# Two-layer hybrid diffusion block: one gate-rank projection, attention output per head, waits per chunk, x loaded in halves, a biased exponent on ScalarE, a paced plan

## The reference, cut to what matters

```
h  = rmsnorm(x, g1) * (1 + sc1) + sh1                 # sc1, sh1: silu(c) @ ada_w + ada_b
z  = h @ w_in   -> pool, q, k, v, r, lr_f(16), lr_b(16), q_dn, kv_dn, k_rope, gates
log_gate(lr, d) = log_sigmoid(lr @ gate_w[d] + gate_b[d]) / 16      # d = forward, backward
gla, per chunk of 64 tokens:
    b = cumsum(g);  qe = q exp(b);  ke = k exp(-b);  kd = k exp(b_last - b)
    o = mask(qe ke^T) v + qe S;   S = exp(b_last) S + kd^T v
mla: softmax((qn kn^T + qr kr^T) * scale) v          # 8 heads; latents read 512 keys, context 256
x  = x + g1 * (sigmoid-gated sum of three branches @ w_out)
h2 = rmsnorm(x, g2) * (1 + sc2) + sh2
peer: q = h2 @ wq; scores against 2 x 128 keys; top 16 of 16 x 16; for each token and head
      16 experts:  sum_j softmax_j * gelu(h2 . u[e_j]) * v[e_j]
x  = x + g2 * peer
```

## Time and profile before

| what | value |
|---|---|
| median of 3 runs | 3509.55 us (3503.07 to 3510.31) |
| the profiled execution: its own time, its span | 3512.18 us, 3510.2 us |
| PE busy | 2868.5 us (82%) |
| DVE, ACT, POOL busy | 1751.3 us (50%), 1083.8 us (31%), 862.1 us (25%) |
| moved | 1071.64 MB, mean 305 GB/s, of which the gathers 805.36 MB |
| mean granted clock of TensorE | 0.890 |
| chain that ended last | PE 53%, DMA 26%, DVE 10%, ACT 6% |

### The profile page before, as it was taken

How to read it: one execution, slowest core, us unless ns; L and a number is a source line. 1 busy time by engine, 2 the same in 40 slices (tenths; PEclk the granted TensorE clock), 3 DMA queues, 4 the chain that set the end, 5 groups by cost and what they waited for, 6 DMA issues and landing times.

```text
span 3510.2 us, 42731 instructions
## 1 busy us (share of the span) xinstructions
PE 2868.5 (82%) x16338; PEld 1793.2 (51%) x16338; DVE 1751.3 (50%) x4345; ACT 1083.8 (31%) x3065; POOL 862.1 (25%) x772
## 2 busy tenths in 40 slices
PE   7999998988898999988776555699999985566555
PEld 5787887654555666664332111278888741111111
DVE  1323013557676555556676766423300256667664
ACT  1222102243555444323433323222310123222232
POOL 0000000323233333323334444200000034444442
PEclk9999999999999999999877867799999987767776
DMA  8654441988898999989989999732144199999996
GB/s 324 273 204 157 156 152 61 379 345 337 347 373 325 420 416 421 384 338 365 386 327 410 415 410 414 300 120 87 70 155 147 72 376 415 411 411 410 410 412 278
DMA packets 151107, 1071.64 MB, mean 305 GB/s; under 512 B 16564, under 2 KB 18228, under 8 KB 22520
## 3 DMA queue, kind: packets, MB, share of 16 engines
q0 software_dynamic: 110592, 805.36, 57.0%
q1 hardware_dynamic: 40312, 263.56, 19.6%
HBM read 1067.80 MB, written 1.05 MB: 304 GB/s over the span
## 4 chain that ended last, share of the span: by engine, by line
PE 53%; DMA 26%; DVE 10%; ACT 6%; issue 3%; POOL 2%; DVEq 0%; ACTq 0%; SPq 0%; POOLq 0%
PE bank L388 39%; DMA ring<-in_experts,eid 25%; PE bank L402 11%; DVE ring L1357 5%; POOL ring L1782 2%; ACT topk_work L909 1%; PE bank L484 1%; ACT topk_work L902 1%; ACT topk_work L899 1%; PE bank L415 1%; DVE state L1547 1%; ACT L899 1%; ACT h_even L967 0%; DVE topk_work L1327 0%; PE bank L608 0%
## 5 line engine op out<-in xcount | busy, mean ns | idle before, releaser
L1782 POOL DMA_INDIRECT ring<-in_experts,eid x768 | 861.9, 1122 | 2611.1 <-PE bank L402 1317.2
L402 PE MATMUL bank<-ring,topk_work 64*64 64x512 f32 x6144 | 992.8, 775 | 542.9 <-ACT topk_work L909 539.1
L1357 DVE CUSTOM_DVE_ANT_0 ring<-ring,h2tok 128x1024 f32<-128x1024 f32 x768 | 936.6, 1224 | 591.7 <-DMA ring<-in_experts,eid 583.4
L402 PEld LDWEIGHTS bank<-ring,topk_work 64*64 64x64 f32 x6144 | 237.3, 160 | 1189.7 <-ACT topk_work L909 888.3
L899 ACT ACTIVATE topk_work<-topk_work 128x2 f32<-128x2 f32 x384 | 77.9, 203 | 1153.1 <-DVE topk_work L1357 1152.5
L388 PE MATMUL bank<-h_even,weights 128*128 128x256 f32 (+1 forms) x1360 | 313.8, 390 | 11.7 <-ACT h_even L967 11.7
L388 PEld LDWEIGHTS bank<-h_even,weights 128*128 128x128 f32 (+1 forms) x1360 | 252.0, 187 | 79.1 <-issue 26.4
L388 PE MATMUL bank<-h_odd,weights 128*128 128x256 f32 (+1 forms) x1056 | 241.5, 385 | 0.8 <-DVE h_even L1566 0.8
L909 ACT ACTIVATE topk_work<-const,topk_work 128x64 f32<-128x64 f32 x768 | 226.0, 341 | 0.4 <-ACT topk_work L902 0.4
L388 PEld LDWEIGHTS bank<-h_odd,weights 128*128 128x128 f32 (+1 forms) x1056 | 196.2, 189 | 57.1 <-issue 26.9
L902 ACT ACTIVATE topk_work<-topk_work 128x1 f32<-128x1 f32 x768 | 184.6, 287 | 12.6
(11 more groups left out here) (230 smaller groups left out, 3096.3 us busy)
## 6 DMA issues: line engine op xcount, KB each, us to landing
weights<-in_quads SPq DMA_DIRECT2D x150, 1024.0 KB, 7.6
ring<-in_quads SPq DMA_DIRECT2D x85, 1024.0 KB, 4.8
ring<-in_experts,eid POOLq DMA_INDIRECT x768, 8.7
ring<-in_quads SPq DMA_DIRECT2D x6, 768.0 KB, 4.2
weights<-in_quads SPq DMA_DIRECT2D x6, 768.0 KB, 6.1
weights<-in_quads SPq DMA_DIRECT2D x12, 256.0 KB
xT<-in_xT SPq DMA_DIRECT2D x1, 2048.0 KB, 11.0
out<-h_even SPq DMA_DIRECT2D x1, 1024.0 KB, 4.5
```

The lines of the kernel that those rows point to most:

```text
L402: x = nc.tensor.matmul(acc[g][out, :], diag[mine, J % 4, :], ring[mine, J % RING, D + h * 512:D + (h + 1) * 512], start=first, stop=J % TI ...
L1357: v.tensor_tensor_reduce(row, row, h2tok[:, u // UNITS % 2, :], 1.0, 0.0, ALU.mult, ALU.add, dots[:, u % 2, j:j + 1]).then_inc(S["dot_done ...
L1782: pool.indirect_dma_start(ring[:, J % RING, :], None, d["experts"], bass.IndirectOffsetOnAxis(eid[:, u % 2, j:j + 1], 0)).then_inc(gathere ...
```

## The change

- **Gate ranks.** The 32 rank columns of both directions are projected as one job, and the gate weights have 33 rows, with zeros for the other direction.
- **Attention.** The order of steps is head by head, both tiles of a head after each other. `weigh` takes one head and both tiles, 256 columns, on every second step; `att_out` copies 256 columns.
- **Waits.** The projection of the ranks and `turn_h2` wait for each chunk of `h` before its own matmul, not for all 8 first.
- **x.** The context half of x is loaded first; the latents' half comes after the 8 modulation quads. The modulation's scale quads (2, 3) come before its shift quads (0, 1), and DVE scales between them.
- **Gla.** ACT copies b_last / 16 to `ends` and takes exp(-b/16 + ends) itself in 8 instructions of 64 columns, straight from PSUM. DVE's copy and subtraction go.
- **State.** For latents (s = 1) the last update of the state of each direction (units 2 and 3, second half) is left out, since nothing reads it.
- **Plan.** `pace` is 0.1 from the start of pass 1 to its queries.

```diff
-PACE = 1.0
+BESIDE, PACE = 0.1, 1.0
-MOD_FIRST = [(0, q) for q in range(4)]
+MOD_FIRST = [(0, q) for q in (2, 3, 0, 1)]
+        ends = sb("ends", [P, 3, GLA_H, 2])
-        lr17 = E[0:RANK + 1, 2560:3072].rearrange("p (d t) -> p d t", d=2)
+        ranks = E[0:2 * RANK + 1, 2560:2816]
         def att_units():
-            return [(t, h) for t in range(2) for h in range(MLA_H)]
+            return [(t, h) for h in range(MLA_H) for t in range(2)]
+        def increments(s, u):
+            return 1 if s and u >= 2 else 2
# SP
-            sp.dma_start(XT[:], ...)
+            sp.dma_start(XT[:, :, span(0)], xT[:, :, span(0)]).then_inc(x_landed, 16)
+            for order, (key, n, slot, done) in enumerate(quads_of):
+                if order == 2 * len(MOD_FIRST):
+                    sp.dma_start(XT[:, :, span(1)], xT[:, :, span(1)]).then_inc(x_landed, 16)
# PE
                     for k in range(nk):
+                        if ready:
+                            pe.wait_ge(*at("h", ready, n, k))
-                    for m in range(2):
+                    for m in range(increments(p.s, u)):
-                def weigh(m): ... x = mm(b[:, 0:P], v, probT[m % 2][:, k, :], ...)
+                def weigh(h):
+                    for t in range(2):
+                        pe.wait_ge(*at("evicted", "pt", n, 2 * h + t))
+                    b = job("ao", n, h)
+                        x = mm(b[:, 0:TS], v, probT[h % 2][:, k, :], k == 0, k == nk - 1)
-                    if m >= 1:
-                        weigh(m - 1)
+                    if m and m % 2 == 0:
+                        weigh(m // 2 - 1)
-                for k in range(DC):
-                    pe.wait_ge(*at("h", "norm1", n, k))
-                project(n, "lr", w, [(0, 0, RANK), (1, RANK, RANK)], h_of(n), DC)
+                project(n, "lr", w, [(0, 0, 2 * RANK)], h_of(n), DC, ready="norm1")
                     for c in range(4):
+                        if t == 0:
+                            pe.wait_ge(*at("h", "norm2", GROUP_PASS[g], m * 4 + c))
-                            cur["pace"] = PACE if g == 1 else 0.0
+                            cur["pace"] = (0.0, PACE, 0.0)[g]
+                if n == 1:
+                    cur["pace"] = BESIDE
# ACT
+                    if p.n == 0 and name == "norm1" and c % 4 == 0:
+                        act.wait_ge(*at("evicted", "mod", 0, 2 * SH1 + c // 4))
-                    act.wait_ge(*at("bdiff", n, u))
-                    nc.scalar.activation(gla_buf(u, GD), gla_buf(u, GD), ACT.Exp, scale=1.0 / TAU)
+                    nc.scalar.activation(ends[...], last_of(b, u), ACT.Copy, scale=1.0 / TAU)
+                    act.wait_ge(*at("ends", n, u))
+                    for h in range(GLA_H):
+                        for c in range(2):
+                            mine = slice(c * CHUNK, (c + 1) * CHUNK)
+                            x = nc.scalar.activation(gla_buf(u, GD)[:, h, mine], bv[:, h, mine], ACT.Exp,
+                                                     scale=-1.0 / TAU, bias=ends[:, u % 3, h, c:c + 1])
# DVE
-                def scale_keys_first(u): ... L1494, L1497, before carry(u - 1, 0)
+                    rows_before("b", n, u)          # in scale_keys, then the wait for ACT
-                        carry(u - 1, 1)
+                        if increments(s, u - 1) == 2:
+                            carry(u - 1, 1)
-                    if m >= 1:
-                        att_out(m - 1)
+                    if m and m % 2 == 0:
+                        att_out(m // 2 - 1)
-                    for i, q in MOD_FIRST:
+                    for i, q in MOD_FIRST[:2]:
                         mod_out(i, q)
                     dve.wait_ge(*at("amod", 0, 0))
                 scale_rows("norm1", 0, p, rstd1[:, :])
+                    for i, q in MOD_FIRST[2:]:
+                        mod_out(i, q)
```

More of the change, by code:

```diff
@@ L230, in build @@
         prob = E[:, 0:1024].rearrange("p (n t) -> p n t", n=2)
-        probT = (E[:, 1024:1536].rearrange("p (k t) -> p k t", k=4), E[:, 1536:2048].rearrange("p (k t) -> p k t", k=4))
+        probT = [E[:, m:m + 1024].rearrange("p (k t) -> p k t", k=4) for m in (1024, 2048)]
         merge_tmp = E[:, 0:512].rearrange("p (n t) -> p n t", n=2)
@@ L324, in _ @@
             sp.dma_start(vec[:], d["vec"]).then_inc(const_landed, 16)
-            sp.dma_start(XT[:], d["xT"].rearrange("(c p) t -> p c t", p=P)).then_inc(x_landed, 16)
+            xT = d["xT"].rearrange("(c p) t -> p c t", p=P)
+            sp.dma_start(XT[:, :, span(0)], xT[:, :, span(0)]).then_inc(x_landed, 16)
             last, loads = {}, {}
-            for key, n, slot, done in quads_of:
+            for order, (key, n, slot, done) in enumerate(quads_of):
+                if order == 2 * len(MOD_FIRST):
+                    sp.dma_start(XT[:, :, span(1)], xT[:, :, span(1)]).then_inc(x_landed, 16)
                 if slot in last:
@@ L454, in square_sums, with project @@
                 return b
-            def project(n, name, w, chunks, src, nk, rows=True):
+            def project(n, name, w, chunks, src, nk, rows=True, ready=None):
                 for c, off, m in chunks:
@@ L609, in turn @@
                     full(x, "pt", n, m)
-                def weigh(m):
-                    t, h = au[m]
-                    pe.wait_ge(*at("evicted", "pt", n, m))
-                    b = job("ao", n, m)
+                def weigh(h):
+                    for t in range(2):
+                        pe.wait_ge(*at("evicted", "pt", n, 2 * h + t))
+                    b = job("ao", n, h)
                     for k in range(nk):
                         v = (VVctok if k < 2 else VVltok)[:, k % 2, h * MV:h * MV + MV]
-                        x = mm(b[:, 0:P], v, probT[m % 2][:, k, :], k == 0, k == nk - 1)
-                    full(x, "ao", n, m)
+                        x = mm(b[:, 0:TS], v, probT[h % 2][:, k, :], k == 0, k == nk - 1)
+                    full(x, "ao", n, h)
                 pe.wait_ge(*at("evicted", "krd", n))
@@ L642, in gate_logits @@
                 w = quad(i, "gate", k=2)
+                pe.wait_ge(*at("evicted", "lr", n, 0))
                 for dd in range(2):
-                    pe.wait_ge(*at("evicted", "lr", n, dd))
                     for t in range(2):
                         b = job("z", n, dd, t)
-                        x = mm(b[:, :], lr17[:, dd, tokl(t)], w[:, dd, :], True, True)
+                        x = mm(b[:, :], ranks[:, tokl(t)], w[:, dd, :], True, True)
                         full(x, "z", n, dd, t)
@@ L815, in queries @@
                 breathe(8.0)
-                for k in range(DC):
-                    pe.wait_ge(*at("h", "norm2", n, k))
                 if g == 1:
@@ L1075, in mixer @@
                     copy_out(kvd[:, c, :], b[:, 0:TS], "kvd", n, c)
-                act.wait_ge(*at("full", "s", n, 2, 1, 1))
+                act.wait_ge(*at("full", "s", n, 2, increments(s, 2) - 1, 1))
                 if p.full:
@@ L1157, in turned @@
                     b = bank_of("pt", n, m)
-                    if m >= 2:
-                        act.wait_ge(*at("full", "ao", n, m - 2))
-                    copy_out(probT[m % 2][:, 0:nk, :], b[:, 0:nk * P].rearrange("p (k t) -> p k t", k=nk), "pt", n, m)
+                    h, t = divmod(m, 2)
+                    if h >= 2 and t == 0:
+                        act.wait_ge(*at("full", "ao", n, h - 2))
+                    copy_out(probT[h % 2][:, 0:nk, tokl(t)], b[:, 0:nk * P].rearrange("p (k t) -> p k t", k=nk), "pt", n, m)
                 expo(0)
@@ L1459, in mixer @@
                 n, i, s = p.n, p.i, p.s
-                v.memset(lr17, 1.0).then_inc(*mark("dve_step", ("lr1", n)))
+                v.memset(ranks, 1.0).then_inc(*mark("dve_step", ("lr1", n)))
                 dve.wait_ge(*at("lr1", n))
-                for dd in range(2):
-                    b = bank_of("lr", n, dd)
-                    copy_out(lr17[0:RANK, dd, :], b[0:RANK, 0:TS], "lr", n, dd)
+                b = bank_of("lr", n, 0)
+                copy_out(ranks[0:2 * RANK, :], b[0:2 * RANK, 0:TS], "lr", n, 0)
                 beside(n, "lr")
@@ L1577, in mixer @@
                         mask(u)
-                    if 0 < u < len(units) - 1:
-                        scale_keys_first(u + 1)
                     if u >= 1:
@@ L1876, in layout @@
         put((i, "lr"), tiled(w[:, 4096:4128]))
-        put((i, "gate"), np.concatenate([a["gla_gate_w"][i], a["gla_gate_b"][i][:, None, :]], 1).transpose(1, 0, 2))
+        gate = np.zeros((2 * RANK + 1, 2, GLA_H * DK), np.float32)
+        for dd in range(2):
+            gate[dd * RANK:(dd + 1) * RANK, dd] = a["gla_gate_w"][i][dd]
+            gate[2 * RANK, dd] = a["gla_gate_b"][i][dd]
+        put((i, "gate"), gate)
         for name, first, count in (("p", 0, 4), ("q", 1024, 2), ("k", 1536, 2), ("v", 2048, 4), ("r", 3072, 4)):
```

44 lines of the change are left out of this document (17 added, 27 removed).

## The result

The changed kernel took 3472.79 us (median of 4 runs, 3470.91 to 3475.70) against 3507.91 for the kernel before (4 runs, 3503.07 to 3510.31) beside it: ratio 0.9896, 95% interval 0.9875 to 0.9918, some 35 us faster. Forecast was 3487, range 3467 to 3506. Run again in experiment 5, the same kernel took 3478.75, ratio 0.9922, 0.9901 to 0.9943. The two intervals overlap; by the two ratios the gain is 27 to 36 us.

What follows compares the result with a forecast made beforehand. PE's own sequence was taken to bound passes 0 and 3, PE and DMA both nearly full beside rows, gathers where rows run alone. Terms summed to -22.3 us: 3490 from the profiled 3512.2, 3487 against the median; range 3467 to 3506.

Steps and rivals of the forecast that it cites:

- Opening, -8.0 forecast: Start of pass 0: ranks start 6.0 us earlier, fewer rank matmuls save 3.5, slow clock costs 1.5; bounds -6 and -12.
- the term for the clock: Opening: more work falls into the 1.2 GHz time at 32 to 46 us, costing 1.5 us.
- the prediction's signs of being wrong: x's first half after 10 us, clock low until 50 us, or PE's diagonal waits in pass 1 up over 15 us.
- Attention of pass 0, +2.0: Two attention steps take 4.02 us for 3.76, eight times, so 2.0 us are lost; bounds 0 and +3.
- Gla, +0.3 and -0.6: Moving the exponents to ScalarE loses 0.3 us in pass 0 and gains 0.6 in pass 3; bounds -2 and +2.
- Norm2, -1.5 twice: Waits per chunk let 7 of 8 transposes finish early, gaining 1.5 us each in pass 0 and at pass 3's end.
- Pass 3, -7.6 from norm1 to norm2: Pass 3: ranks and norm1 gain 6.5 us, gla 0.6 and attention 0.5.
- Pass 1, -4: Beside rows in pass 1: 3 us gained by work removed, 1 by the plan; the plan's bounds are -12 and +15.
- the plan -1: Pass 1: `pace` moves about one pair of rows forward out of the merge, gaining 1 us.
- the slower rival: Pass 1: pace moves 4 to 5 pairs that stall PE, losing 32 us, total 3525; chance 0.08, half of it slower.
- the faster one: Pass 1: pace pays, earlier rows fill idle DMA and 14 us more go, total about 3471; chance 0.14.
- Pass 2, -2: Pass 2: the ranks' 3.5 us go where PE has 70 us idle, gaining 2 us; bounds -5 and +3.

Runs made afterwards that it cites:

- experiment 5: The changed kernel run again unchanged, beside the kernel before: 3478.75 us, ratio 0.9922.
- experiment 7: The kernel before with only the biased exponents on ScalarE added: 3495.32 us, ratio 0.9977 against the kernel before.
- experiment 12: The kernel before with the single rank job, biased exponent on ScalarE and left-out state updates: 3487.79 us, ratio 0.9953 against the kernel before.
- experiment 1: The changed kernel with a pace of 0 instead of 0.1 beside pass 1: 3482.03 us, ratio 0.9943 against the kernel before.
- experiment 8: The changed kernel with x loaded in one transfer, new quad order kept: 3477.71 us, ratio 0.9932 against the kernel before.
- experiment 9: The changed kernel with the four modulation quads in the old order 0, 1, 2, 3: 3476.62 us, ratio 0.9913 against the kernel before.

## Why the prediction was right, point by point

- **Opening, -8.0 forecast.** The first k matmul came 11.7 us earlier (10.8 to 11.9 in the six other executions with all of the opening's parts), not 8.0. The ranks start 7.1 us earlier for 6.0, and from there to k 4.6 us are gained for 2.0. The mechanism was right; the term for the clock was wrong in sign. I gave +1.5 because more work would fall into the slow time at 32 to 46. The slow time moved with the work, to 25.4 to 35.6, and was 10.2 us for 13.7. Of the parts: the rank job 2.1 (51.24 to 49.11 between experiments 7 and 12, in spite of 6.8 us more slow clock), and everything else, 8.1 (49.1 to 41.0), hangs on waits and order together. Each alone recovers most: without the new order 0.9 is lost, without the waits by chunk 2.7. Halves of x are 0.7. None of the prediction's signs of being wrong showed: x's first half was there by 9.2 us (10), the clock was back at 35.6 (50), and PE's waits for the diagonals in the first part of pass 1 went from 48.9 to 50.3 us (15 more).
- **Attention of pass 0, +2.0.** +2.2, with the forecast's steps to the hundredth (2.29; 1.70 for 1.73).
- **Gla, +0.3 and -0.6.** Between 0 and -1.7 in pass 3 (experiment 7). Eight exponents take 1.75 us, my low end was 2.0. They are 1.2 us more than the one of 512 columns (0.59), where the smaller estimate that the prediction mentions had 0.4 more.
- **Norm2, -1.5 twice.** -1.7 in place at pass 3's end. In pass 0 from scaling to the first gather 28.2 us are left for 27.7 when half the slow time is taken off: nothing reached the rows.
- **The whole of pass 0** to the first gather: forecast -7.2. Measured -15.9, of which 8.5 is the clock (30.7 us slow before, 13.7 after, at half cost); -7.4 is left. That the sum came out is partly luck: the opening gave some 2 us more than forecast even with its own clock taken off, norm2 gave 2 less. And the two profiled executions differ by as much again in clock.
- **Pass 3, -7.6 from norm1 to norm2.** -5.2 in the profiled execution; 494.9 us, -7.4, in experiments 1, 5, 8 and 9. Slow clock is 6.8 us before, 9.1 changed and 3.4 in those four; less half of it, -6.3 and -5.7. Up to the reciprocal of gla's norms: 177.6 before, 174.4 with the ranks and the exponent (experiment 12), 169.3 with the waits too (experiments 1, 5, 8 and 9); with slow clock of 6.8, 10.2 and 3.4 us in them, a part of each step is the clock. The ranks' copy 6.5 earlier was exact. The term for the attention, -0.5, was +0.9. I had read PE as the bound from one step in the middle, which has no gap. In the last two steps PE waits for the other engines, 2.0 us before and 3.1 changed.
- **Pass 1, -4.** Measured is 0 (881.5 to 881.3 us less half the slow time), so the step that failed would be "the plan -1" and with it "-3 work off PE". But single executions lie in 876.5 to 885.7 by this measure, too wide to tell 0 from -4. The rows moved further than I planned: the last gather came 853.6 us after the first, and 853 us after its own first gather the kernel before stood at gather 247 of 256, so it is four to five pairs and not one. Neither rival's price came: no stall (the slower rival), nothing paid (the faster one). The rows ended early, and norm2, the queries and the choice of rows of the latents were the last wait.
- **Pass 2, -2.** The term that was mis-sized most: -11 (mean of ten against four), with the traces pointing at VectorE's queue in gla. I counted 3.5 us of PE's time at a little over half with 70 us idle and left VectorE's relief of 1.3 us a unit at nothing, although showed VectorE waiting for the decay and the rows' dot products stand in the same queue.

So -22.3 became -27 to -36. The excess is pass 2 (9 us) and less slow time ahead of the rows; pass 1's 4 us are missing. The largest parts by whole times: the rank job (ratio 0.9988 without it for 0.9922, 23 us, of which its stages show some 16: 1.6 in the opening, 11 in the second group, 3.5 in pass 3; 0.9977 to 0.9953, 8 us, when it joins the exponent alone), the exponent (8 us alone, 8 lost without it), the waits by chunk (0.9950 without for 0.9922, 10 us). Only two of these are clear of noise by their intervals: the rank job's 23 us, and the exponent alone, 2 to 14 us below before. The others' intervals overlap with those that they are compared with. The attention per head costs 3 us by stage, and pace and halves of x bring nothing that a time shows. What the left-out updates of state bring was not tried by itself. The parts overlap and don't add.

## What to carry to other kernels

Before costing a removed instruction by its own time, look at what is queued behind it on its engine when it waits: here 1.4 us a unit on VectorE, with a rank job on PE, went with 11 us less in the second group, where gathers were three hand-overs behind. Rows brought forward by 35 us gained nothing, since the latents' own work ended the stretch; find first what ends last. A copy that depends on the newest result of another engine is worth trying one step later in its queue: in pass 0 it turned a loss of 2.2 us into a gain of 1.8. And one step without a gap does not speak for a whole stage: look at its last steps too, where there is nothing left to fill the wait (pass 3: 3.1 us of idle PE, 1.0 with the later copy).

## What the runs showed of the hardware that was not expected

- The same code differs by 9 us in one stretch of some 900, and the time at the granted clock of 1.2 GHz goes with it: 0.54 us longer per us at 0.50 granted, correlation 0.91 over 14 profiled executions (of 13 kernels), 41 to 75 us of slow time. In 55 executions of the kernel before (3491 to 3523 us, mean granted clock 0.893 to 0.907) time and clock correlate with -0.64. A stretch less half of its slow time lies in 876.5 to 885.7 for all 14, where the stretches themselves spread over 901.8 to 919.9.
- The slow time in the opening came earlier when PE's work did: 32.3 to 46.0 before, 25.4 to 35.6 after (29 to 46 in the three executions with the old opening, 24 to 41 in the eleven with a changed one). At the gate logits (about 82 to 101 us) it came in some executions of the same kernel and not in others.
- Eight ScalarE exponents of 64 columns from PSUM with a bias per partition take 1.75 us, 0.22 from start to start; one of 512 columns takes 0.59.
- Half of x in pieces of 1 KB (2563 packets under 2 KB for 496) left the rate of the first 40 us at 378 GB/s for 380.
